# Expert stage of a two-block transformer: weights in whole tiles, four tiles held back in the lead places, and tokens picked by products

## The chip, the cores and the metric

The kernel runs on one core of one Trainium2 chip. The metric is the device time of one execution in microseconds. The core has five engines with instruction streams of their own: TensorE (PE; its weight loads are the rows PEld), VectorE (DVE), ScalarE (ACT), GpSimd (POOL) and SyncE (SP). SyncE and GpSimd issue the transfers here.

## The reference

Two blocks over 256 tokens of width 1024, in float32: HGRN2 and RG-LRU mixing, attention, two feed-forward layers with convolution; then latent attention, a dense SwiGLU, an S5 mixer, and a mixture of experts. Only the last is touched:

```python
def moe_swiglu(h, w_router, w_gate, w_up, w_down):
    t = h.reshape(B * S, D)                        # 256 x 1024
    logits = (t @ w_router).astype(jnp.float32)    # 8 experts
    top_vals, top_idx = lax.top_k(logits, TOP_K)   # TOP_K = 2
    gates = jax.nn.softmax(top_vals, axis=-1)
    combine = jnp.sum(jax.nn.one_hot(top_idx, N_EXPERTS, dtype=jnp.float32) * gates[..., None], axis=1)
    out = jnp.zeros_like(t)
    for e in range(N_EXPERTS):                     # D_FF_EXPERT = 3584
        he = swiglu(t, w_gate[e], w_up[e], w_down[e])
        out = out + combine[:, e:e + 1].astype(t.dtype) * he
    return out.reshape(B, S, D)
```

The input of this step is the RMS norm of the residual with a gain; the residual is added to it, and a last RMS norm with `final_norm` follows.

## The kernel before

Ahead of the experts all weights stream through four slots of 24 KB per partition (`SLOTS`), each unit loaded by SyncE as `slot_free` tells that its slot is empty. The experts follow: each of the 8 has 28 tiles (`FE_TILES`) of 128 hidden channels. A tile has a gate-and-up part of 8 KB per partition (`UP`) and a down part of 4 KB (`DOWN`), 1.5 MB in all, 224 tiles together.

Each token goes to 2 of 8 experts, and an expert computes only the tokens sent to it, at most `CAP` = 88 (if one gets more, a flag `crowded` sends all engines into a dense path, `experts_dense`, that these inputs don't take). TensorE counts each token's place in its expert by products (`router`); VectorE turns this to `posm`, and `picks` makes from it, for one expert, a matrix of 256 x 88 that has the token's inverse norm where token and place agree. `gather` multiplies the tokens `vtok` by it: 32 products of 64 output rows by 88 columns (each appears twice in the trace, so 64 records) leave the chosen tokens in PSUM, transposed as the tiles want them. VectorE's `take_input` scales them to `xg`.

Before the change only experts 0 and 1 get their tokens so, both ahead of the first tile (L1813). For experts 2 to 7, GpSimd scatters all normalized rows (`hrow`, from VectorE, L2743) into a table in HBM, `rows_in`, by four indirect transfers (L573), then loads 88 rows of one expert at a time to `xl` (L567), and TensorE turns them by `turn_rows` (L1826), 32 records, behind the last tile of an expert. `rows_in` is filled with zeros at the program's start (L550, eight stores of 352 KB).

For one tile, `up` (L1866) makes gate and up by 64 records, ScalarE takes Silu of the gate, VectorE multiplies (L2698, `hid_ready`), and `down` (L1882), 32 records, adds into the expert's sums in PSUM, then raises `moe_free`. The order is up of tile f + 1, down of tile f. `four` is four tiles; the first four are written out, the others run in loops. Behind an expert, VectorE copies the sums out (L2705), `open_sums` (L1905) clears them, `turn_sums` (L1835) turns them, and GpSimd stores 88 rows of results to `rows_out` (L583). In the last expert four indirect gathers bring the results back by token (L586, `returned`), and VectorE weighs and adds them.

Where the weights lie: the first four tiles use two of the slots, the lead places. All others go through a ring of four places in the two other slots (`RING`), the up parts and the down parts of a place apart. SyncE refills the up part when `up_ready` tells that its products are done, the down part on `moe_free`:

```python
with sp.Fori(2, last) as i:
    for h in range(RING):
        sp.wait_ge(up_ready, i * (2 * RING) + (2 * (FT0["moe"] + h - RING) + 4))
        load_up((h + 1) % RING, i * RING + (h + 1))
        sp.wait_ge(moe_free, i * RING + h + 1)
        load_down(h, i * RING + h)
```

The lead places hold no further weights afterwards; `hrow`, `xl` and `returned` lie there. Ahead of `gather`, TensorE also spreads the final norm's gains over the partitions by eight products (L1711), and ScalarE copies them out (L1015).

Of the kernel before, what the change touches and what calls it, by code (L numbers as in the profile page):

```python
# [43 lines left out]
RING = 4  # L44
GROUPS = FE_TILES // RING
WEIGHTED_AT = 16
RETURN_AT = 16
ZEROED = 16 * (EXPERTS + 3)
# [120 lines left out]
def build_program(nc, a):  # L169

    ctx = ExitStack()
    with ctx:
# [31 lines left out]
        rows_in = nc.dram_tensor("rows_in", (EXPERTS * T, D), F32, kind="Internal").ap()  # L204
# [59 lines left out]
        def gate_up(f, k):  # L264
# [50 lines left out]
        moe_up_loaded = [sem(f"moe_up_loaded{i}") for i in range(RING)]  # L315
        moe_down_loaded = [sem(f"moe_down_loaded{i}") for i in range(RING)]
# [4 lines left out]
            "scattered", "loaded", "ystored", "returned")}  # L321
# [45 lines left out]
        def mid(k, n):  # L367
# [26 lines left out]
                  for i in (*range(0, 12, 2), *range(20, 34, 2))]  # L394
# [6 lines left out]
        first_picks = [part(i)[:, 0:2 * CAP].rearrange("p (g n) -> p g n", g=2) for i in (22, 23)]  # L401
# [28 lines left out]
        lead_slots, ring_slots = ([(len(LOADED) - SLOTS + k) % SLOTS for k in some]  # L430
                                  for some in ((0, 1), (2, 3)))

        def up_places(two):
            return [slots[two[h // 3]][:, h % 3 * UP:(h % 3 + 1) * UP] for h in range(RING)]

        def down_places(two):
            return [slots[two[1]][:, UP + h * DOWN:UP + (h + 1) * DOWN] for h in range(RING)]

        lead_loaded = [_n[k] + 16 * n for k, n in zip(lead_slots, (3, 1 + RING))]

        lead_ups, lead_downs = up_places(lead_slots), down_places(lead_slots)
        ups, downs = up_places(ring_slots), down_places(ring_slots)

        lead = [slots[k] for k in lead_slots]
        hrow = lead[0][:, 0:2 * D].rearrange("p (g d) -> p g d", g=2)
        xl = lead[0][0:CAP, 2 * D:3 * D]
        returned = lead[1][:, 0:4 * D].rearrange("p (n d) -> p n d", n=4)
        where = part(25)[:, 16:64].rearrange("p (n c) -> p n c", c=8)
        slot_row, back_row = idx[:, 0, 0:4], idx[:, 0, 4:8]
# [6 lines left out]
        def _(sp):  # L456
# [39 lines left out]
            def load_up(h, unit):  # L496
                sp.dma_start(ups[h], a["w_moe"][bass.ds(unit, 1), :, 0:UP].rearrange(
                                 "o p n -> p (o n)")).then_inc(moe_up_loaded[h], 16)
# [17 lines left out]
            for h in range(RING):  # L516
                load_down(h, RING + h)
# [2457 lines left out]
```

## Time and profile before

| | us |
|---|---|
| median of 3 runs | 2178.97 |
| lowest, highest | 2176.01, 2182.1 |
| the profiled execution | 2182.77 |
| its span, first to last instruction | 2180.7 |
| TensorE busy | 2114.9 |
| VectorE busy | 837.9 |
| ScalarE busy | 465.8 |
| GpSimd busy | 24.7 |

The span ends 2.1 us short of the execution's time. The expert stage begins at about 1290 us of the span with the first `gather` and ends near 2168 us, so it is two fifths of the time. Busy times are of the whole span: TensorE is busy 97% of it, which does not tell whether a matmul waited for its weights for a little before each tile. That has to be read from the distance of the starts, and that of the DMA engines from their share in a window.

### The profile page before, as it was taken

What the parts mean: (1) busy time and instruction counts of PE and PEld (TensorE: products, weight loads), DVE (VectorE), ACT (ScalarE), POOL (GpSimd) and SP (SyncE); (2) the same over time, 40 slices, a digit from 0 to 9 for tenths busy, and PEclk for the clock granted to TensorE, in tenths of its full rate; (3) what the DMA queues carried; (4) which work ended last, traced back from release to release, by engine and by line L of the source; (5) the groups of instructions that cost most, each with busy time, mean ns of one, the idle gap of its engine ahead of it and who ended that gap; (6) DMA issues with size and microseconds to landing.
All of it is one profiled execution on the core that took longest, in us unless ns stands there. A gap on an engine that the chain in (4) does not pass through costs nothing.

```text
span 2180.7 us, 67375 instructions
## 1 busy us (share of the span) xinstructions
PE 2114.9 (97%) x30418; PEld 1945.7 (89%) x30418; DVE 837.9 (38%) x2085; ACT 465.8 (21%) x1074; POOL 24.7 (1%) x43
## 2 busy tenths in 40 slices
PE   9999999999999999999997899999999999999998
PEld 8889999856999986899986789999999999999997
DVE  4357676314766655467759520101010101010102
ACT  3432112113311134211023221111111111111112
POOL 1000000000000000000000000000000000000000
PEclk9999999999999999999998999999999999999999
DMA  9241444240334423324431338999999999999997
GB/s 394 93 173 72 162 174 175 81 169 8 139 150 169 160 97 136 155 117 174 168 142 40 116 117 327 413 416 410 418 410 418 409 418 409 418 417 416 418 417 287
DMA packets 78407, 534.35 MB, mean 245 GB/s; under 512 B 9106, under 2 KB 9235, under 8 KB 41939
## 3 DMA queue, kind: packets, MB, share of 16 engines
q1 hardware_dynamic: 74450, 519.82, 59.3%
q0 software_dynamic: 3840, 12.85, 1.6%
q8 instruction: 89, 1.46, 0.3%
q14 instruction: 28, 0.22, 0.0%
HBM read 523.00 MB, written 9.63 MB: 244 GB/s over the span
## 4 chain that ended last, share of the span: by engine, by line
PE 65%; DMA 4%; DVE 2%; ACT 1%; issue 1%; DVEq 0%; SPq 0%; ACTq 0%
PE ps L1866 24%; PE ps L1224 12%; PE ps L1882 11%; PE ps L1266 7%; DMA slot<-in_w_moe 4%; PE ps L1141 4%; PE ps L1633 2%; PE ps L1616 1%; DVE scr L2549 0%; PE ps L1813 0%; PE ps L1157 0%; PE ps L1503 0%; PE ps L1489 0%; PE ps L1096 0%; PE ps L1570 0%
## 5 line engine op out<-in xcount | busy, mean ns | idle before, releaser
L1866 PE MATMUL ps<-scr,slot 128*64 128x88 f32 x14336 | 595.4, 241 | 11.1 <-issue 5.4
L1866 PEld LDWEIGHTS ps<-scr,slot 128*64 128x64 f32 x14336 | 562.8, 137 | 22.1 <-issue 12.4
L2698 DVE TENSOR_TENSOR scr<-scr,ps 128x88 f32<-128x88 f32 x224 | 55.1, 246 | 727.1 <-ACT scr L982 727.1
L1882 PE MATMUL ps<-scr,slot 128*64 128x88 f32 x7168 | 315.5, 239 | 1.9 <-issue 1.9
L1882 PEld LDWEIGHTS ps<-scr,slot 128*64 128x64 f32 x7168 | 292.0, 137 | 5.1 <-issue 5.1
L1266 PE MATMUL ps<-scr,slot 128*128 128x256 f32 x1056 | 237.6, 380 | 1.6 <-DVE scr L2369 1.6
L1266 PEld LDWEIGHTS ps<-scr,slot 128*128 128x128 f32 x1056 | 196.6, 191 | 26.0 <-DVE scr L2369 2.0
L982 ACT ACTIVATE scr<-ps 128x88 f32<-128x88 f32 x224 | 54.5, 243 | 743.8 <-PE ps L1866 743.8
L1224 PE MATMUL ps<-vtok,slot 128*128 128x128 f32 x1056 | 139.6, 275 | 0.0
L1224 PEld LDWEIGHTS ps<-vtok,slot 128*128 128x128 f32 x1056 | 128.8, 192 | 0.2
L1224 PE MATMUL ps<-vtok,proj 128*128 128x128 f32 x1056 | 128.7, 275 | 0.0
L1224 PEld LDWEIGHTS ps<-vtok,proj 128*128 128x128 f32 x1056 | 123.2, 192 | 0.0
L1224 PEld LDWEIGHTS ps<-hT,slot 128*128 128x128 f32 x960 | 116.2, 192 | 2.8
L1224 PE MATMUL ps<-hT,slot 128*128 128x128 f32 x960 | 116.9, 275 | 0.0
L1141 PE MATMUL ps<-hT,slot 128*128 128x256 f32 x416 | 95.7, 389 | 0.6 <-PE ps L1141 0.6
L2295 DVE TENSOR_TENSOR proj<-slot 128x512 f32<-128x512 f32 x132 | 91.1, 690 | 6.2 <-ACT mixT L746 2.9
L839 ACT ACTIVATE sq<-ps 128x128 f32<-128x128 f32 x66 | 18.3, 277 | 351.3 <-PE ps L1224 351.3
L1141 PEld LDWEIGHTS ps<-hT,slot 128*128 128x128 f32 x416 | 80.4, 196 | 13.9 <-issue 3.1
L1320 PE MATMUL ps<-hT,slot 128*128 128x256 f32 x384 | 86.5, 384 | 2.0 <-DMA slot<-in_w_even_in 1.7
L1141 PE MATMUL ps<-mixT,slot 128*128 128x256 f32 x384 | 84.6, 381 | 1.3 <-PE ps L1141 0.9
L1320 PEld LDWEIGHTS ps<-hT,slot 128*128 128x128 f32 x384 | 73.5, 193 | 13.2 <-DMA slot<-in_w_even_in 2.0
L1141 PEld LDWEIGHTS ps<-mixT,slot 128*128 128x128 f32 x384 | 72.5, 190 | 12.9 <-issue 3.0
(412 smaller groups left out, 2058.4 us busy)
## 6 DMA issues: line engine op xcount, KB each, us to landing
slot<-in_w_moe SPq DMA_DIRECT2D x224, 1024.0 KB, 12.2
slot<-in_w_moe SPq DMA_DIRECT2D x224, 512.0 KB, 12.2
slot<-in_w_ffn SPq DMA_DIRECT2D x33, 3072.0 KB, 10.8
slot<-in_w_even_in SPq DMA_DIRECT2D x3, 3072.0 KB, 27.2
slot<-in_w_odd_qk SPq DMA_DIRECT2D x2, 3072.0 KB, 10.6
slot<-in_w_s_glu SPq DMA_DIRECT2D x2, 3072.0 KB, 11.9
slot<-in_w_odd_v SPq DMA_DIRECT2D x2, 2048.0 KB, 8.4
slot<-in_w_even_in SPq DMA_DIRECT2D x2, 1536.0 KB, 10.6
```

Source lines behind the costliest of these rows:

```text
L839: act.activation(mid(k, 0), product(k, P1), ACT.Copy).then_inc(first_copied, 1)
L982: act.activation(gbuf[j][:, 0:CAP], gate_up(j, 0), ACT.Silu).then_inc(gate_act, 1)
L1141: m = pe.matmul(ps[:, bank0 + n % ring, 0:T], w[:, o:o + P], src[:, c], start=c == 0, stop=c == k - 1, skip_group_check=True)
L1224: m = pe.matmul(product(k, n), weights[:, c * P:(c + 1) * P], x[:, c], start=first and c == 0, stop=c == 3, skip_group_check=True)
L1266: m = pe.matmul(acc(d), w[:, o:o + P], hid2[u % 2][:, half], start=u == half == 0 and d % 2 == 0, stop=last, skip_group_check=True)
L1320: m = pe.matmul(even_tile(i), project.w[:, o:o + P], hT[:, c], start=c == 0, stop=c == KD - 1, skip_group_check=True)
L1616: m = pe.matmul(ps[k:k + 32, q % 2, a:b], w[:, r, q, k:k + 32], x[:, j, 0:n], start=False, stop=i == 3, skip_group_check=True)
L1633: m = pe.matmul(glu_tile(i), w[:, o:o + P], hT[:, c], start=c == 0, stop=c == KD - 1, skip_group_check=True)
L1866: m = pe.matmul(gate_up(j, k)[s:s + STRIP], w[:, o:o + STRIP], xg[:, c], start=c == 0, stop=c == KD - 1, skip_group_check=True)
L1882: m = pe.matmul(y_sum(d)[s:s + STRIP], w[:, o:o + STRIP], hid[j][:, 0:CAP], start=False, stop=False, skip_group_check=True)
L2295: dve.tensor_tensor(dst, a, b, ALU.subtract).then_inc(combined, 1)
L2698: dve.tensor_tensor(hid[f % 4][:, 0:CAP], gbuf[f % 4][:, 0:CAP], gate_up(f, 1), ALU.mult).then_inc(hid_ready, 1)
```

## The change

- Both parts of a tile are one transfer of 12 KB per partition (`load_tile`), with one semaphore per place. There are eight places, two in each slot. A place is free when its down products are done (`moe_free`).
- The four lead places (0 to 3) take tiles 0 to 3, and once used, the last four tiles, 220 to 223. The ring (4 to 7) takes all others.
- `gather` serves every expert. VectorE makes the picks for expert e + 2 at the ninth tile of expert e (`PICKS_AT` = 8) in one buffer. `gather` for expert 1 stands behind the first four tiles, the others where `turn_rows` stood.
- `rows_in`, its zeros, the scatter, the loads, `hrow`, `xl` and the row numbers for it are gone. `returned` is spread over four free buffers.
- In the router, four filler products (`busy(4, 5)`) take the place of the eight for the final norm's gains, which stand behind the counting of places; ScalarE copies them after its Exp, and TensorE waits for these copies later.
- The dense path is rewritten for the same places.

```diff
-            for h in range(RING):
-                for s in lead_slots[0:1 if h < 3 else 2]:
-                    sp.wait_ge(slot_free, left(s))
-                sp.dma_start(lead_ups[h], a["w_moe"][h, :, 0:UP]
-                             ).then_inc(slot_loaded[lead_slots[h // 3]], 16)
...
+            def load_tile(h, unit):
+                sp.dma_start(places[h], a["w_moe"][bass.ds(unit, 1), :, :].rearrange(
+                                 "o p n -> p (o n)")).then_inc(moe_loaded[h], 16)
+
+            for h in range(PLACES):
+                sp.wait_ge(slot_free, left(tile_slots[h]))
+                load_tile(h, h)
             for h in range(RING):
...
+                sp.wait_ge(moe_free, RING + h + 1)
+                load_tile(h, TILES - RING + h)
+            with sp.Fori(2, TILES // RING - 1) as i:
                 for h in range(RING):
...
                     sp.wait_ge(moe_free, i * RING + h + 1)
-                    load_down(h, i * RING + h)
+                    load_tile(RING + h, i * RING + h)
...
-            for e in range(EXPERTS):
-                pool.dma_start(rows_in[e * T:e * T + CAP, :], no_rows).then_inc(mo["scattered"], 16)
...
-            for n in range(4):
-                pool.indirect_dma_start(
-                    out=rows_in, out_offset=bass.IndirectOffsetOnAxis(ap=slot_row[:, n:n + 1], axis=0),
-                    in_=hrow[:, n // 2], in_offset=None).then_inc(mo["scattered"], 16)
-            pool.wait_ge(mo["scattered"], ZEROED + 16 * 4)
-            load(2)
...
-                def turn_rows(loads):
-
-                    pe.wait_ge(mo["loaded"], loads)
...
-                gather(0)
-                gather(1)
-                up(0, None, 1)
+                gather(2, picks_of[0], 0)
+                up(0, 0, 16, 1)
                 open_sums(None)
                 four(0, 0, first=True)
+                gather(4, picks_of[1])
                 with pe.Fori(1, GROUPS) as i:
                     four(0, i)
-                turn_rows(16)
+                gather(6, picks_of[1])
                 open_sums(2)
+                pe.wait_ge(fin["rowtaken"], 2)
                 turn_sums(2)
...
-                with pe.Fori(0, GROUPS - 1) as i:
+                with pe.Fori(0, GROUPS - 2) as i:
                     four(EXPERTS - 1, i)
-                four(EXPERTS - 1, GROUPS - 1, True)
+                four(EXPERTS - 1, GROUPS - 2, before_last=True)
+                four(EXPERTS - 1, GROUPS - 1, last=True)
...
+                        if e < EXPERTS - 2 and f == PICKS_AT:
+                            dve.wait_ge(mo["gathered"], 2 * (e + 1) + 2)
+                            picks(e + 2, picks_of[1])
```

How this moves instructions, at three places. On TensorE at the stage's start, before: L1711 are the gains' products, L1718 to L1723 count places, L1946 is the branch on `crowded`, L1813 is `gather`, L1866 the first tile.

```order
L1711 MATMUL ps<-cst,vec 128x128 x8
L1718 MATMUL ps<-scr,cst 128x16
L1721 MATMUL ps<-scr,ones 128x8 x2
L1723 MATMUL ps<-scr,ones 128x8
L1946 TENSOR_LOAD crowded
L1946 ISA x2
L1946 COMPARE_AND_BRANCH
L1813 MATMUL ps<-scr,vtok 64x88 x64
L1866 MATMUL ps<-scr,slot 64x88 x32
```

The same place in the changed kernel, where L1074 are the filler products, L1671 the gains' and L1761 is `gather`.

```order
L1074 MATMUL ps<-cst,ones 128x256 x4
L1663 MATMUL ps<-scr,cst 128x16
L1666 MATMUL ps<-scr,ones 128x8 x2
L1668 MATMUL ps<-scr,ones 128x8
L1671 MATMUL ps<-cst,vec 128x128 x8
L1877 TENSOR_LOAD crowded
L1877 ISA x2
L1877 COMPARE_AND_BRANCH
L1761 MATMUL ps<-scr,vtok 64x88 x32
L1798 MATMUL ps<-scr,slot 64x88 x32
```

The gains' products moved between the counting and the branch, and 32 products of `gather` stand ahead of the first tile in place of 64. On TensorE between the last tile of an expert and the next expert's loop, before: L1826 is `turn_rows`, L1905 `open_sums`, L1835 `turn_sums`.

```order
L1913 COMPARE_AND_BRANCH
L1826 MATMUL ps<-cst,slot 64x88 x16
L1905 MATMUL ps<-cst 128x1 x2
L1835 MATMUL ps<-cst,scr 88x128 x8
L1918 UNCONDITIONAL_BRANCH
```

The same in the changed kernel.

```order
L1843 COMPARE_AND_BRANCH
L1761 MATMUL ps<-scr,vtok 64x88 x32
L1835 MATMUL ps<-cst 128x1 x2
L1771 MATMUL ps<-cst,scr 88x128 x8
L1849 UNCONDITIONAL_BRANCH
```

16 products that read the loaded rows became 32 that read the tokens and the picks. On SyncE's queue, the expert weights up to the ring's loop and its first turn, before (ring slots 3 and 0).

```order
L507 DMA slot1<-in_w_moe 128x2048 [waits slot_free] x3
L507 DMA slot2<-in_w_moe 128x2048 [waits slot_free]
L510 DMA slot2<-in_w_moe 128x1024 x4
L497 DMA slot3<-in_w_moe 128x2048 [waits slot_free] x3
L497 DMA slot0<-in_w_moe 128x2048 [waits slot_free]
L501 DMA slot0<-in_w_moe 128x1024 x4
L497 DMA slot3<-in_w_moe 128x2048 [waits up_ready]
L521 UNCONDITIONAL_BRANCH
L521 ISA
L497 ISA [waits up_ready]
L497 DMA slot3<-in_w_moe 128x2048
L501 ISA [waits moe_free]
```

And in the changed kernel.

```order
L488 DMA slot1<-in_w_moe 128x3072 [waits slot_free] x2
L488 DMA slot2<-in_w_moe 128x3072 [waits slot_free] x2
L488 DMA slot3<-in_w_moe 128x3072 [waits slot_free] x2
L488 DMA slot0<-in_w_moe 128x3072 [waits slot_free] x2
L488 DMA slot1<-in_w_moe 128x3072 [waits moe_free] x2
L488 DMA slot2<-in_w_moe 128x3072 [waits moe_free] x2
L497 UNCONDITIONAL_BRANCH
L497 ISA
L488 ISA [waits moe_free]
L488 DMA slot3<-in_w_moe 128x3072
```

Every load after the first eight now waits for `moe_free` alone, and the four for the lead places (slots 1 and 2) stand ahead of the ring's.

## Rows read from the trace of the kernel before

**Rows 1.** The page: span, and the expert weights among the DMA issues (KB, us to landing).

```profile
span 2180.7 us, 67375 instructions
...
slot<-in_w_moe SPq DMA_DIRECT2D x224, 1024.0 KB, 12.2
slot<-in_w_moe SPq DMA_DIRECT2D x224, 512.0 KB, 12.2
```

**Rows 2.** Windows: stretch, length, busy PE PEld DVE ACT POOL, clock, DMA share, GB/s.

```profile
1300.00:1304.00 4.00, 4.00 (x98) 3.88 (x96) 0.25 (x1) 0.49 (x2) 0.00 (x0) 1.00 0.01 4
1400.00:1500.00 100.00, 98.31 (x2546) 97.44 (x2544) 9.41 (x32) 15.32 (x33) 1.05 (x2) 1.00 1.02 414
```

**Rows 3.** Timeline of TensorE in expert 1: start, us, then line and operation.

```profile
1428.75 2.66 PE L1866 MATMUL ps<-scr,slot 128*64 128x88 f32 x64
...
1494.27 2.66 PE L1866 MATMUL ps<-scr,slot 128*64 128x88 f32 x64
```

**Rows 4.** The chain that ended last, in order of time, in expert 5: start, us.

```profile
1917.10 2.65 PE ps L1866 x64
...
1947.23 2.65 PE ps L1866 x64
```

**Rows 5.** Timeline of VectorE: the copies of an expert's sums, five of eight ends.

```profile
1409.46 0.96 DVE L2705 COPY scr<-ps 128x440 f32<-128x440 f32 x2 [3.95 <-PE ps L1882]
...
1842.77 0.95 DVE L2705 COPY scr<-ps 128x440 f32<-128x440 f32 x2 [4.02 <-PE ps L1882]
...
1951.14 0.96 DVE L2705 COPY scr<-ps 128x440 f32<-128x440 f32 x2 [4.01 <-PE ps L1882]
...
2058.25 0.95 DVE L2705 COPY scr<-ps 128x440 f32<-128x440 f32 x2 [3.95 <-PE ps L1882]
...
2167.58 0.62 DVE L2705 COPY scr<-ps 128x440 f32<-128x440 f32 x1 [1.91 <-PE ps L1882]
```

**Rows 6.** Timeline of TensorE around the end of expert 0.

```profile
1401.71 2.65 PE L1866 MATMUL ps<-scr,slot 128*64 128x88 f32 x64
...
1409.24 1.39 PE L1826 MATMUL ps<-cst,slot 88*64 88x88 f32 x32
1410.56 0.61 PE L1905 MATMUL ps<-cst 128*128 128x1 f32 x4
...
1415.70 2.60 PE L1866 MATMUL ps<-scr,slot 128*64 128x88 f32 x64
```

**Rows 7.** Timeline of TensorE: stalls; in brackets the idle time and its end.

```profile
1329.09 0.24 PE L1866 MATMUL ps<-scr,slot 128*64 128x88 f32 x1 [2.48 <-issue]
...
1426.72 1.05 PE L1866 MATMUL ps<-scr,slot 128*64 128x88 f32 x21 [1.02 <-issue]
...
2086.41 2.65 PE L1866 MATMUL ps<-scr,slot 128*64 128x88 f32 x64 [2.25 <-DMA slot<-in_w_moe]
```

**Rows 8.** Transfers: SyncE's first weights; their landings; window 8:14; 1500:1510; a lone load.

```profile
2.67 0.56 SPq L463 DMA_DIRECT2D slot<-in_w_even_in  x1
3.28 0.47 SPq L464 DMA_DIRECT2D slot<-in_w_even_in  x1
...
DMA to landing us min/median/max: 9.0/9.0/9.0
...
DMA to landing us min/median/max: 12.1/12.1/12.1
...
DMA packets 226, 2.58 MB, mean 430 GB/s; under 512 B 16, under 2 KB 16, under 8 KB 16
...
DMA to landing us min/median/max: 12.1/12.2/12.2
...
slot<-in_w_mla_uk SPq DMA_DIRECT2D x1, 1024.0 KB, 4.8
```

**Rows 9.** The two picks ahead of the first tile, and a window in them.

```profile
1290.21 7.96 PE L1813 MATMUL ps<-scr,vtok 128*64 128x88 f32 x128 [1.76 <-DVE scr L2663]
...
1290.00:1292.00 2.00, 1.79 (x24) 1.80 (x26) 1.50 (x8) 1.77 (x3) 0.00 (x0) 0.50 1.03 422
```

More of the change, by code:

```diff
@@ L320, in build_program @@
             "yetaken", "yturned", "yeready", "spread", "weighted", "pturned", "rows",
-            "scattered", "loaded", "ystored", "returned")}
+            "scattered", "ystored", "returned")}
         out_turned, out_stored = sem("out_turned"), sem("out_stored")
@@ L428, in build_program @@
         mix0 = {"even_out": 0, "odd_out": KD, "mla_o": 2 * KD}
[L430 to L447, printed above, removed]
+        tile_slots = [(len(LOADED) - SLOTS + h // 2) % SLOTS for h in range(PLACES)]
+        places = [slots[s][:, h % 2 * (UP + DOWN):(h % 2 + 1) * (UP + DOWN)]
+                  for h, s in enumerate(tile_slots)]
+        ups, downs = [x[:, 0:UP] for x in places], [x[:, UP:UP + DOWN] for x in places]
+        returned = [yT[:, 4:8].rearrange("p a n -> p (a n)"),
+                    xbp[:].rearrange("p a n -> p (a n)")[:, 0:D],
+                    rgw[:].rearrange("p k j n -> p (k j n)"), part(34, 4)]
         where = part(25)[:, 16:64].rearrange("p (n c) -> p n c", c=8)
-        slot_row, back_row = idx[:, 0, 0:4], idx[:, 0, 4:8]
+        back_row = idx[:, 0, 4:8]
         no_rows = mixT[0:CAP, 0:4].rearrange("p a n -> p (a n)")
@@ L516, in _ @@
-            for h in range(RING):
-                load_down(h, RING + h)
-            last = EXPERTS * FE_TILES // RING - 1
-            sp.wait_ge(up_ready, 2 * (FT0["moe"] + RING) + 2)
-            load_up(0, 2 * RING)
-            with sp.Fori(2, last) as i:
+            def load_tile(h, unit):
[4 more added lines that the diff above has]
+                load_tile(h, h)
@@ L1709, in router @@
                 pe.wait_ge(tile_taken, TILE0["s5_glu"] + 2 * KD)
-                for c in range(KD):
-                    m = pe.matmul(ps[:, 6 + c // 4, c % 4 * P:c % 4 * P + P],
-                                  v("final_norm", c).to_broadcast([P, P]), ident, start=True, stop=True,
-                                  skip_group_check=True)
-                    if c % 4 == 3:
-                        m.then_inc(fin["row"], 1)
+                busy(4, 5)
                 pe.wait_ge(mo["sel"], 2)
@@ L1789, in expert @@
                         down(f)
-                expert(0, True)
-                with pe.Fori(1, EXPERTS) as e:
-                    expert(e, False)
+                expert(0, first=True)
+                with pe.Fori(1, EXPERTS - 1) as e:
+                    expert(e)
+                expert(EXPERTS - 1, last=True)
                 pe.wait_ge(moe_free, RING + EXPERTS * FE_TILES)
@@ L1803, in experts_gathered, with gather @@
             def experts_gathered():
-                def gather(e):
-                    pe.wait_ge(mo["pick"], 2 * e + 2)
+                def gather(picks, picked, bank0=2):
+                    pe.wait_ge(mo["pick"], picks)
                     for b in range(2):
```

169 lines of the change are left out of this document (62 added, 107 removed).

## The prediction

> **What bounds the kernel now.** I read the page first: a span of 2180.7 us, and 224 tiles of expert weights, each in two transfers of 1024 and 512 KB that take 12.2 us to land [rows 1]. The table of windows then shows the expert stage: TensorE busy 98.3 of 100 us and the DMA engines at share 1.02 with 414 GB/s in the same stretch, while from 1300 to 1304 us, when the stage has begun, they move nothing (share 0.01) [rows 2]. So two limits lie on top of each other, and the question is which one is late where. The timeline of TensorE answers it. Where the weights are there, a tile (16 column blocks of gate and up, 8 of down) starts every (1494.27 - 1428.75) / 18 = 3.64 us [rows 3]. Later, in the chain that ended last, eight tiles take 1947.23 - 1917.10 = 30.13 us, 3.77 us each [rows 4]. 1.573 MB in 3.766 us is 417.6 GB/s: there the weight stream sets the pace, 0.126 us a tile above TensorE's own. The copies of an expert's sums, one at each expert's end, give the periods: (2058.25 - 1409.46) / 6 = 108.13 us in the mean for experts 1 to 6, 107.11 for expert 6 alone, 108.37 for expert 5, and 109.33 for the last [rows 5]. The 3.64 us pace alone would be 28 x 3.64 = 101.9.
>
> The rest of a period is the pause between experts and stalls. The pause: three tiles around it take 1415.70 - 1401.71 = 13.99 us, 3.07 more than 3 x 3.64 [rows 6]; of that the turning of the loaded rows (L1826, 32 records) takes 1.32, from 1409.24 to 1410.56 with the next line's start. The stalls: TensorE sits with nothing awaited (the page's "issue") for 1.02 us at 1426.7 and 2.48 us at 1329.1, both in the first tiles after the code leaves one piece and enters another, and 2.25 us for a weight tile at 2086.4, just after the four gathers of returned rows were issued [rows 7].
>
> **The weight stream, part by part.** Before, a period moves 28 tiles, one load and one store of 88 rows. Expert 6's period (107.11) has no load, expert 5's (108.37) has: 352 KB on the GpSimd queue cost 1.26 us of stream [rows 5]. 28 x 3.766 + 2 x 1.26 = 108.0 against the mean of 108.13: these periods are the stream's. 
>
> After: no loads of rows. And a tile is one transfer with 12 KB for each partition in place of 8 + 4. What that does to the rate, the trace shows only nearby: the two first loads, 1536 KB each with 12 KB per partition, were issued at 2.67 and 3.28 us and landed 9.0 and 12.1 us later [rows 8], so at 11.67 and 15.38, 3.71 us apart. That bounds it from above at 3.71; the window from 8 to 14 us, with big packets only, has 430 GB/s [rows 8], 3.66 us a tile. If nothing changes, it stays 3.77; as the lowest I allow 3.62, an estimate 1% under the window. I take 3.67, next to the window, since its packets are the big ones and nothing else is in it.
>
> **The ring.** Before, the gate-up part of a place was refilled as soon as its products were done. From there to its next use lie 4 x 3.64 - 2.43 = 12.1 us, and in the paced stretch a load takes 12.1 to 12.2 us to land [rows 8]: the window is used up exactly. After, the whole place waits for the down products, and its next use comes two tiles later, 7.28 us. A lone 1024 KB load lands in 4.8 us [rows 8]; 512 KB more at 418 GB/s make 6.1, with 0.2 to issue 6.3. The slack is 1.0 us. Hence the stream can't be more than 1 us ahead after an expert's pause, and whatever it falls behind by more, TensorE waits for. The Trainium skill's same page ("Anatomy of one DMA") has a fixed 2.0 us plus bytes / 436e3, an estimate of 5.6 us and 0.5 us more slack; the landings speak for 6.1.
>
> **TensorE, part by part.** The products that pick tokens (L1813) replace the turning of rows: 64 records against 32. At the start 128 of them took 7.96 us [rows 9], but at a granted clock of 0.50, that is 1.2 GHz, after an idle of 1.76 us. Records of the same shape (64 columns by 88) in a tile take 2.43 / 64 = 0.038 us each at full clock, so a pick is 2.43, and the pause grows by 2.43 - 1.2 = 1.2 us, to 4.3. I take that, with 3.98 as the other end (a pick at half clock). It happens behind experts 0 to 5; VectorE writes the picks at the ninth tile, two small operations for each, and is busy only 9.4 of 100 us in the stage [rows 2], so they are there long before. The pick for expert 1 also moves, from ahead of the first tile to behind the fourth: 2.43 there.
>
> Now by stretch:
> - *Stage start to the end of expert 0*, 1290.21 to 1409.46, 119.25 us: 7.8 of picks, 101.9 of tiles, 0.6 of opening, 8.9 of stalls, among them the 2.48. After: one pick at the start instead of two (-3.98), but the eight products of the final norm's gains now stand ahead of the register load and the branch, which used to run within the 1.76 us that TensorE idled for the picks (between 0 and +1.76, taken as +1.2); half clock reaches into the first tile (+1.0); the pick for expert 1 (+2.43). The scatter and its 2 MB fall away, yet the stream, which moved nothing from 1300 to 1304 us [rows 2], is full from the first freed place on, and instructions are fetched beside it; I give 2.4 of the 8.9 back, between 0 and 6. Sum -1.8 (from -5.4 with full clock and few stalls to +1.6).
> - *Six periods to the end of expert 6*: TensorE 101.9 + 4.3 + stalls of about 1.0 (one like that of 1.02 us in expert 1 for each, between 0 and 2 of them) = 107.2. Stream: 28 x 3.67 + 4.3 - 1.0 of slack = 106.1, plus 1.26 for the store, of which a part falls into the stall, 106.7. They lie close and do not overlap fully: 107.4. Six make 644.4 against 648.79: -4.4 (from -8 at 3.62 to +1 at 3.72).
> - *The last expert*: the picks' growth doesn't apply, the turning of the placement stays. 109.33 is 101.9 + 3.1 + 2.25 for the wait on the returned rows and 2.1 of pace. After: the wait stays, the pace goes but for 0.03 x 20 = 0.6 over the tiles ahead of the last four, which lie in place already, and the stall of 1.0 that the old pace hid may show in part or not. Between -2.8 and 0, I take -2.1.
> - *Elsewhere*: the eight stores of zero rows at 26 us at the program's start go; the weights needed then were ahead of them on the rings, so nothing. The gain rows' copy on ScalarE moves behind Exp, and ScalarE has nothing to do until the first tile's gate. The four returned buffers lie elsewhere in SBUF, no cost. The stage's end, 2167.6 to 2180.7, stays.
>
> Sum -1.8 - 4.4 - 2.1 = -8.3 us. The execution profiled took 2182.77, 3.8 above the median of 2178.97 and 2.1 above its span; I put the difference on the median: 2170.7, **2171 us** (a span near 2172.4). What is odd here: an earlier stream in bigger packets and no row loads is worth little, since TensorE's own work is only 1 to 2 us a period shorter than the stream's before, and the picks take most of that back.
>
> **The rivals.**
> *Shallow ring, no faster packets (slower).* If a tile still takes 3.77, then the period is 28 x 3.766 + 4.3 - 1.0 = 108.7, and some of the store on top, 109.0: +0.9 in six, +5.4; the first stretch +1.5, the last expert 0 to +0.5. In all +7, 2186. It decides from 3.72 us a tile on, where 28 x 3.72 + 3.3 + 0.7 gives the present 108.1. For it: 12 KB packets beside a full TensorE appear nowhere. Against: 3.71 and 430 GB/s. Chance 0.13.
> *Everything cancels.* Stalls for code grow, since the loops are entered over more straight code, and each late tile costs in full at 1 us of slack: +1.2 a period instead of a gain of 0.7, first stretch +1: near 2179. Chance 0.20.
> *Stalls mostly vanish.* They came while the stream was full; after the change it often rests, above all in the pauses. Then 106.3 a period (-11), first stretch -4, last -3: 2161. Chance 0.17.
> *The ring isn't rearranged as said* (a tile waits for lead places): the order rows show the lead places refilled ahead of the ring's first, which delays tile 8 only if four loads take longer than four tiles, 14.7 against 14.6 + 2.4. No case of its own.
>
> **How the numbers follow.** Forecast 0.50, around 2171 (its own range 2164 to 2178). 0.3% is 6.5 us, about what a measurement of this kernel can tell from no change: faster is below 2172.4, slower above 2185.5. Of the forecast's half, 0.31 lies below and 0.19 within; with 0.17 of the vanishing stalls faster is 0.48; within 0.19 + 0.18 + 0.03 = 0.40; slower 0.10 + 0.02 = 0.12. The range takes the forecast and both near rivals and reaches to the slow one: 2160 to 2186.
>
> **What would show it.** Right: landings of 1536 KB at 6 to 7 us, DMA share in the stage near 0.97 to 1.0, tiles 3.64 us apart in every expert, periods of 107 to 108 us with a pause of 4.3, first tile near 1296. Wrong: tiles 3.75 apart and waits on the weights after each pause (the slower rival), picks at 0.062 us a record (half clock in the pauses), or many idles without a releaser.

## The result, and the profile after

The changed kernel takes 2263.05 us (median of 4, 2259.01 to 2267.0) where the kernel before, beside it on the chip, takes 2178.21: a ratio of 1.0387, 95% interval 1.0361 to 1.0414. It is slower by 85 us, far outside the range; the slow rival had the right sign with a tenth of the size.

The page of the changed kernel. From section 1's head, section 4, section 5 and section 6, the lines that answer to [rows 1]; the last two columns of section 5's line are the busy time with the mean of one in ns, and the idle time ahead of them with what ended it:

```profile
span 2263.8 us, 67094 instructions
...
L1798 PE MATMUL ps<-scr,slot 128*64 128x88 f32 x14336 | 590.7, 240 | 74.2 <-DMA slot<-in_w_moe 70.3
...
slot<-in_w_moe SPq DMA_DIRECT2D x224, 1536.0 KB, 8.4
```

TensorE sat idle for 70.3 us for expert weights; before it was 4.1. The rest of the 83.1 us of span is mostly in its busy time, which grew by 18.4 us, from 2114.9 to 2133.3: behind a wait the first part of a tile takes 2.65 us in place of 2.43, as the chain below shows. The waits of TensorE in the stage (us in total, times, longest) and the windows that answer to [rows 2]:

```profile
PE ps L1798 <- DMA slot<-in_w_moe: 70.3, 96, 2.0
```

```profile
1400.00:1500.00 100.00, 91.44 (x2288) 88.23 (x2284) 9.14 (x31) 12.03 (x28) 0.52 (x1) 1.00 0.94 364
```

96 small waits, none above 2.0 us, and the stream at 364 GB/s where [rows 2] had 414. The DMA engines' share is 0.94: they are neither full nor resting for long. This points at a ring that is too shallow, not at a stream that is too heavy; the experiments test it. The landings, first of the three loads issued at 1303.6, 1307.2 and 1310.8 us (the first, into an empty queue, took 6.7 us, the next two 8.2 and 9.3), then of the 23 issued from 1400 to 1500 (they answer to [rows 8]):

```profile
DMA to landing us min/median/max: 6.7/8.2/9.3
```

```profile
DMA to landing us min/median/max: 7.7/8.4/10.1
```

The chain of waits in expert 0 (start, us) shows what a refill costs TensorE, from the issue to the first product:

```profile
1323.81 2.43 PE ps L1798 x64
...
1331.26 8.71 DMA slot<-in_w_moe
...
1340.02 2.65 PE ps L1798 x64
...
1344.05 8.29 DMA slot<-in_w_moe
```

Timeline of VectorE, the copies of an expert's sums, as in [rows 5] (experts 0, 6 and 7):

```profile
1420.78 0.95 DVE L2634 COPY scr<-ps 128x440 f32<-128x440 f32 x2 [4.95 <-PE ps L1809]
...
2135.42 0.95 DVE L2634 COPY scr<-ps 128x440 f32<-128x440 f32 x2 [4.03 <-PE ps L1809]
...
2250.69 0.62 DVE L2634 COPY scr<-ps 128x440 f32<-128x440 f32 x1 [1.90 <-PE ps L1809]
```

So the loss by stretch, the third column being an experiment below (gate-up part refilled early):

| stretch, us | before | after | early refill |
|---|---|---|---|
| program's start to the first copy | 1409.46 | 1420.78 | 1408.89 |
| six periods | 648.79 | 714.64 | 638.55 |
| one of them | 108.13 | 119.11 | 106.43 |
| last expert | 109.33 | 115.27 | 107.95 |
| from there to the end | 13.1 | 13.1 | 13.1 |

79% of the loss, 65.85 of 83.1 us, lies in the six periods, 11 us in each. Last, TensorE at the stage's start and around the end of expert 0, as in [rows 9] and [rows 6]:

```profile
1290.11 2.03 PE L1671 MATMUL ps<-cst,vec 128*128 128x128 f32 x16
1292.07 2.65 PE L1761 MATMUL ps<-scr,vtok 128*64 128x88 f32 x64
1296.54 0.68 PE L1798 MATMUL ps<-scr,slot 128*64 128x88 f32 x12 [1.83 <-DVE scr L2611]
...
1420.57 2.60 PE L1761 MATMUL ps<-scr,vtok 128*64 128x88 f32 x64
1423.10 0.60 PE L1835 MATMUL ps<-cst 128*128 128x1 f32 x4
1423.56 1.05 PE L1771 MATMUL ps<-cst,scr 128*88 128x128 f32 x8
1424.55 2.65 PE L1798 MATMUL ps<-scr,slot 128*64 128x88 f32 x64
```

Behind expert 0 the pick runs at full clock and takes 2.53 us to the next line's start, where the turning took 1.32: 1.2 us more, as forecast. From the pick's first product to the next expert's tile are 3.98 us. What failed is the ring.

### The profile page after: what moved, and what is told of

It is laid out like the page before. It is cut to its first block, busy times and chain, and to the rows that moved or that the text cites. A ratio compares the mean times of both kernels' runs of the same rounds, so it can differ in the third digit from the quotient of the medians.

```text
span 2263.8 us, 67094 instructions
## 1 busy us (share of the span) xinstructions
PE 2133.3 (94%) x30618; PEld 1951.5 (86%) x30618; DVE 838.1 (37%) x2094; ACT 466.1 (21%) x1074; POOL 13.4 (1%) x25
## 4 chain that ended last, share of the span: by engine, by line
PE 47%; DMA 22%; DVE 3%; ACT 1%; issue 1%; SPq 0%; DVEq 0%; ACTq 0%
DMA slot<-in_w_moe 22%; PE ps L1798 12%; PE ps L1174 11%; PE ps L1216 7%; PE ps L1809 6%; PE ps L1091 4%; PE ps L1583 2%; PE ps L1761 1%; PE ps L1566 0%; DVE scr L2480 0%; PE ps L1771 0%; PE ps L1107 0%; PE ps L1453 0%; PE ps L1439 0%; PE ps L1520 0%
## 5 line engine op out<-in xcount | busy, mean ns | idle before, releaser
L1798 PE MATMUL ps<-scr,slot 128*64 128x88 f32 x14336 | 590.7, 240 | 74.2 <-DMA slot<-in_w_moe 70.3
L1798 PEld LDWEIGHTS ps<-scr,slot 128*64 128x64 f32 x14336 | 555.2, 137 | 100.0 <-DMA slot<-in_w_moe 66.7
L1809 PE MATMUL ps<-scr,slot 128*64 128x88 f32 x7168 | 310.2, 239 | 0.9 <-issue 0.9
L1809 PEld LDWEIGHTS ps<-scr,slot 128*64 128x64 f32 x7168 | 287.4, 137 | 1.0 <-issue 1.0
L1091 PE MATMUL ps<-hT,slot 128*128 128x256 f32 x416 | 95.4, 388 | 0.7 <-PE ps L1091 0.7
L1270 PE MATMUL ps<-hT,slot 128*128 128x256 f32 x384 | 91.4, 399 | 2.6 <-DMA slot<-in_w_even_in 2.3
L1091 PEld LDWEIGHTS ps<-mixT,slot 128*128 128x128 f32 x384 | 72.4, 190 | 13.1 <-issue 3.0
```

The lines of the kernel that those rows point to most:

```text
L1091: m = pe.matmul(ps[:, bank0 + n % ring, 0:T], w[:, o:o + P], src[:, c], start=c == 0, stop=c == k - 1, skip_group_check=True)
L1270: m = pe.matmul(even_tile(i), project.w[:, o:o + P], hT[:, c], start=c == 0, stop=c == KD - 1, skip_group_check=True)
L1798: m = pe.matmul(gate_up(j, k)[s:s + STRIP], ups[place][:, o:o + STRIP], xg[:, c], start=c == 0, stop=c == KD - 1, skip_group_check=True)
L1809: m = pe.matmul(y_sum(d)[s:s + STRIP], downs[place][:, o:o + STRIP], hid[j][:, 0:CAP], start=False, stop=False, skip_group_check=True)
```

## The experiments

Three theories stood against each other. **A**: the ring is too shallow: too few bytes are in flight, since a place's window, from its refill to its next use, is too short. **B**: transfers of whole tiles in 12 KB rows are slower in themselves. **C**: TensorE's side, picks or code. All times are medians; "ratio" is against the kernel before, run beside it (2176.6 to 2178.4).

### A deeper ring, and the same ring held back

All eight places become one ring; nothing is special about the first or the last four tiles.

```
+            with sp.Fori(1, TILES // PLACES) as i:
+                for h in range(PLACES):
+                    sp.wait_ge(moe_free, i * PLACES + (h - RING + 1))
+                    load_tile(h, i * PLACES + h)
```

TensorE's code has the place of a tile follow from its number modulo eight, so loops of eight tiles are written out in place of four. The two held-back kernels differ from it in one constant, `+ 4` or `+ 5` for `+ 1`.

> The changed kernel with one edit in the order of the weight transfers: the eight places are one ring for all 224 tiles, so a freed place is needed again six tiles later (21.8 us) and not two (7.28 us); transfers stay whole tiles of 12 KB rows, picks stay products. Theory A (too few transfers in flight: a tile's transfer lands 8.2 to 8.4 us after its issue with one other in flight, two tiles per landing make 4.2 us a tile): with six in flight the stream runs at 3.7 to 3.77 us a tile, the periods fall from 119 to 107-109 us and the time to 2150-2180. Theory B (whole-tile transfers with 12 KB rows are slower in themselves): the rate stays at 360 to 390 GB/s, periods stay above 115, time 2230-2265. Theory C (TensorE's side: picks, code): above 2200 with no waits on the weights. My number: 2165.

> The ring of eight places, but each refill waits for four more tiles to be done, so that a place is needed again two tiles after its transfer is issued, as in the changed kernel; nothing else differs from the ring of eight. Theory A: the periods come back to 118-122 us, time 2250-2275 (2263). Theory B: the same as the ring of eight without the wait, whatever that is. Theory C: the same as that too.

> The ring of eight places with refills held back by three tiles: a place is needed again three tiles (10.9 us) after its issue. Theory A: up to three transfers in flight; before, 3.24 tiles in flight made 3.77 us a tile; if landings go as 3 x the tile time, the stream runs at 3.7 to 3.85, periods 108-111, time 2170-2195 (2180). Theory B: the same as the ring of eight. Theory C: the same.

Measured: the ring of eight 2231.92 (ratio 1.0246, 1.0226 to 1.0266), held back by four tiles 2292.63 (1.054, 1.0503 to 1.0577), by three 2226.72 (1.0228, 1.0205 to 1.0251). The first line of TensorE's waits in the stage, of the one held back by four and of the one by three:

```profile
PE ps L1790 <- DMA slot<-in_w_moe: 62.0, 84, 1.9
```

```profile
PE ps L1790 <- issue: 31.3, 25, 5.0
PE ps L1801 <- issue: 18.2, 17, 1.9
```

One tile more of window, 3.64 us, takes 84 waits on weights down to none and 66 us off the time. Code, picks, places and packets are the same in both, so A holds and B falls. With three tiles of window the stream also runs as fast as it can, in the window 1585 to 1625 of the kernel held back by three:

```profile
1585.00:1625.00 40.00, 40.00 (x1062) 40.00 (x1060) 2.71 (x11) 6.54 (x14) 0.00 (x0) 1.00 1.01 426
```

426 GB/s is 3.69 us a tile; the tiles there start 3.64 us apart. But the time I gave, 2165, was missed by 67 us. A new cost had come in with my edit: 31 + 18 us of idle in which TensorE waits for nothing the profile shows. That is taken up below.

### Which part of the ring's change does it

The ring of four was changed in two ways: both parts are refilled at the tile's end, and both are waited for at the tile's start. Four kernels separate the two, with the picks of the changed kernel, and one does the refill alone in the kernel before. First, the changed kernel with two transfers on one semaphore, so that only the packets are those of before:

```
-                sp.dma_start(places[h], a["w_moe"][bass.ds(unit, 1), :, :]...
+                sp.dma_start(ups[h], a["w_moe"][bass.ds(unit, 1), :, 0:UP]...
+                sp.dma_start(downs[h], a["w_moe"][bass.ds(unit, 1), :, UP:UP + DOWN]...
```

> The changed kernel with each tile brought by two transfers (1024 KB in 8 KB rows, 512 KB in 4 KB rows) issued together when its place is free, and waited for together: the changed kernel's window with the packets of before. Theory A (the window alone): time 2250-2270, periods 117-121. Theory B (12 KB rows or whole-tile transfers): back to 2170-2190. Mixed: if the shorter packets spread a tile more evenly over the queue, 2230-2250. My number: 2255.

Measured 2266.01 (ratio 1.0418, 1.0388 to 1.0448), the changed kernel's time. B falls a second time, and from the other side. Next, the same refill with the parts waited for apart:

```
-                def down(j, place, hids):
+                def down(j, place, hids, loads):

+                    if place >= RING:
+                        pe.wait_ge(moe_down_loaded[place], loads)
```

> The changed kernel with the gate-up and the down part of the four ring places brought apart and waited for apart, both refilled together when the place's down products are done. Against the kernel with both parts on one wait (2266 us) only the wait for the down part moves, from ahead of the tile's gate-up products to ahead of its down products, 6.07 us later (two gate-up parts and one down part, 2.43 + 1.21 + 2.43). If the one wait is what costs, the down third of the bytes gains 6.07 us of window (13.35 in place of 7.28) and the time falls to 2172-2190 (2178), as the kernel before with the late refill alone (2187) less the 8.5 us that picks and missing row transfers are worth. If the refill at the tile's end is what costs, 2240-2266.

Measured 2190.62 (1.0052, 1.0034 to 1.0069). Then the early refill, with both waits as before:

```
+                    sp.wait_ge(up_ready, i * (2 * RING) + (2 * (FT0["moe"] + h - RING) + 4))
+                    load_up(RING + (h + 1) % RING, i * RING + (h + 1))
                     sp.wait_ge(moe_free, i * RING + h + 1)
-                    load_tile(RING + h, i * RING + h)
+                    load_down(RING + h, i * RING + h)
```

> The changed kernel with the gate-up part of the four ring places brought apart (8 KB rows) and refilled as soon as its products are done, the down part (4 KB rows) when the down products are done, as the kernel before does; picks as products, no rows loaded or scattered and the lead places used again for the last four tiles stay. Theory A: the stream is back at 418 GB/s, 3.77 us a tile, periods 28 x 3.77 + up to 1.3 for the store = 105.5-107.5, where TensorE's own 101.9 + 4.3 make 106.2: time 2165-2180 (2170), no long waits on the weights. Theory C (picks or code cost it): above 2200.

Measured 2168.18 (0.9956, 0.9942 to 0.997), 0.4% faster than the kernel before. Its gate-up parts land 8.6 us after their issue, in a stream of 418 GB/s from 1500 to 1900 us:

```profile
slot<-in_w_moe SPq DMA_DIRECT2D x106, 1024.0 KB, 8.6
```

And the early refill with one wait for both parts at the tile's start:

> The changed kernel with both parts of the four ring places apart and the gate-up part refilled early (the kernel of 2168 us), but TensorE waits for both parts ahead of the gate-up products. Window of the gate-up part 12.1 us, of the down part 7.28. If what counts is the window weighted by bytes (here 10.5 us; 9.3 held the pace nearly, 7.28 didn't), little is lost: 2168-2185 (2178). If the shortest window of any part counts, with a tile's landing of 8.4 us, 2220-2265.

Measured 2192.14 (1.0064, 1.0042 to 1.0086). TensorE's waits on the weights in these four, in the order told:

```profile
PE ps L1800 <- DMA slot<-in_w_moe: 68.6, 89, 2.5
```

```profile
PE ps L1818 <- DMA slot<-in_w_moe: 10.9, 13, 2.4
```

```profile
PE ps L1829 <- DMA slot<-in_w_moe: 1.2, 1, 1.2
```

```profile
PE ps L1830 <- DMA slot<-in_w_moe: 8.0, 10, 2.6
```

| | two waits | one wait |
|---|---|---|
| gate-up refilled early | 2168.2 | 2192.1 |
| both refilled at the end | 2190.6 | 2266.0 |

Either edit costs 22 to 24 us, both together 98. They don't add. The late refill takes 4.85 us of window from the gate-up part, the early wait takes 6.07 us from the down part, and only when both are gone has every byte of a tile just 7.28 us. The landings fit this: the part that is left with 7.28 us lands 7.2 us after its issue where it is the gate-up part alone, 7.1 where it is the down part alone, and 8.4 where it is the whole tile. So either part alone just about fits the window and the whole tile doesn't. That is read from the landings; no run varies them by themselves.

What the half edits still cost is the pause. In the middle of an expert their stream runs at its full rate, and behind the pause it doesn't, since it had no free place to run ahead into. Early refill with one wait, ten us in the middle of expert 2 and ten just behind the pause after it:

```profile
1590.00:1600.00 10.00, 9.93 (x262) 9.76 (x259) 0.74 (x3) 2.01 (x4) 0.00 (x0) 1.00 1.02 418
1630.00:1640.00 10.00, 10.00 (x250) 9.81 (x250) 1.78 (x4) 0.49 (x2) 0.51 (x1) 1.00 0.94 339
```

Its periods are 109.6 us in the mean, those of the late refill with two waits 110.3: near 28 x 3.766 + 3.98 = 109.4, a stream that sets the pace in the tiles and rests in the pause. My guess that the window weighted by bytes decides is not borne out: 10.5 us of it (early, one wait) is no faster than 9.3 (late, two waits), and they came out 14 and 13 us slower than I had put them.

The late refill alone, in the kernel before:

```
+            with sp.Fori(2, EXPERTS * FE_TILES // RING) as i:
                 for h in range(RING):
-                    sp.wait_ge(up_ready, i * (2 * RING) + (2 * (FT0["moe"] + h - RING) + 4))
-                    load_up((h + 1) % RING, i * RING + (h + 1))
                     sp.wait_ge(moe_free, i * RING + h + 1)
+                    load_up(h, i * RING + h)
                     load_down(h, i * RING + h)
```

> The kernel before with one edit: the gate-up part of a ring place is refilled together with its down part, when the down products are done, as the changed kernel does, and not as soon as the gate-up products are done. Its window shrinks from 12.1 to 7.28 us; row loads, turned rows, 8 + 4 KB rows stay. Theory A (window): the tile time goes to 4.2 us with two tiles in flight, periods 118-123 us, time 2255-2275 (2265), waits on the weights of 60 us and more; this part of the change alone makes the loss. Theory C (the loss is in picks, code or packets of 12 KB): within 10 us of 2178.

Measured 2186.66 (1.0055, 1.0038 to 1.0071), where I expected 2265: a miss, and the most useful one. I had overlooked that the kernel before waits for the down part only ahead of the down products. Its issues from 1400 to 2000 us (KB, median us to landing) show why it nearly suffices; they stand against a window of 7.28 us for the first part and 13.35 for the second:

```profile
slot<-in_w_moe SPq DMA_DIRECT2D x154, 1024.0 KB, 7.2
slot<-in_w_moe SPq DMA_DIRECT2D x154, 512.0 KB, 7.9
```

The late refill costs 10 us here and 22 where the early-refill kernel is the base. That fits the pace: the kernel before already pays the stream's 3.77 us a tile (its periods for experts 2 to 5 are 108.3 to 109.0 us, with the late refill 107.8 to 108.4), while in the early-refill kernel TensorE's 3.64 decides. So the gains of the two can't be added, as I had done for the 2178 above.

### Where the rings of eight lose their gain

The same ring with less code: one loop of eight tiles, run seven times for two experts, with the work between experts inside it behind a condition.

```
+                with pe.Fori(0, EXPERTS // 2) as q:
+                    with pe.Fori(0, FE_TILES // RING) as m:
+                        four(q, m, 0)
+                        with pe.If(m == 3):
...
+                        four(q, m, 1)
```

> The ring of eight places with less code: one loop body of eight tiles is run 7 times for two experts, the work between the experts stands in it behind a condition on the loop's register, and the pick for expert 1 stands ahead of the first tile. The ring of eight (2232) had no waits on the weights but 55 us of idle with nothing awaited, and 59 to 63 instruction packets in 700 us of its stage against 7 of the changed kernel. If that idle is code being loaded (its body of two experts has 24 tiles written out, the changed kernel's 4), it goes with the smaller body: periods 106-108, time 2150-2170 (2158), instruction packets under 15 in the same stretch. If it isn't the size of the code but the entering of loops: the same 2225-2235. If conditions on TensorE are dear, 1 to 2 us each of 28: 2190-2215.

Measured 2201.76 (1.0121, 1.0104 to 1.0138): 30 us less than the ring of eight, neither of the times expected in full. The idle has shrunk to 30.1 us in nine pieces. Six of them, of 3.8 to 4.9 us, come in pairs each time the outer loop turns back to its start, as here in the chain of waits, with the window behind the first; none stands at the condition.

```profile
1509.83 0.92 PE ps L1763 x8
1510.74 4.89 issue
1515.63 4.96 PE ps L1790 x64
...
1535.94 3.75 issue
```

```profile
1515.00:1521.00 6.00, 5.37 (x74) 5.38 (x76) 0.09 (x1) 0.24 (x1) 0.00 (x0) 0.50 0.21 83
```

The clock granted there is 0.50, and 64 records take 4.96 us in place of 2.65. So a turn costs more than its idle: the periods with a turn are 121.49, 119.76 and 119.29 us, those without 105.96 each. Without the 42.7 us of the three turns this kernel would take an estimated 2159 us, which is what was expected of it.

The instruction queue on the page, for the changed kernel, the ring of eight and this one:

```profile
q8 instruction: 93, 1.52, 0.3%
```

```profile
q8 instruction: 160, 2.62, 0.4%
```

```profile
q8 instruction: 105, 1.72, 0.3%
```

To see whether code alone does this, the inner loop of the 2168 us kernel was written out; TensorE's products, the waits and the transfers stay the same:

```
                 with pe.Fori(1, EXPERTS - 2) as e:
-                    with pe.Fori(0, GROUPS) as i:
+                    for i in range(GROUPS):
                         four(e, i)
```

> The kernel of 2168 us (gate-up part refilled early) with one edit on TensorE alone: for experts 1 to 5 the inner loop of seven rounds of four tiles is written out, 28 tiles of code one behind the other, and run once for each expert. Transfers, waits and products are the same. If TensorE's idle in the rings of eight was the loading of code, its idle grows here too: with every tile's code run once for each expert, either 2 to 4 us at each expert's start only, since straight code is fetched ahead (time 2178-2195), or all along, 1 us and more for each four tiles (2200-2240); instruction packets in 600 us of the stage 100 or more against 7. If that idle had to do with the ring of eight and not with code, the time stays 2165-2171. My number: 2200.

Measured 2287.46 (1.0511, 1.0488 to 1.0534), 119 us slower. TensorE's waits in the stage, the instruction queue in the 400 us from 1500 on (1 packet there in the early-refill kernel), the chain at the end of an expert, and the window behind it:

```profile
PE ps L1829 <- issue: 82.1, 61, 4.8
```

```profile
q8 instruction: 73, 1.20, 1.2%
```

```profile
1531.21 1.47 issue
1532.69 2.04 PE ps L1789 x48
1534.73 0.54 PE ps L1868 x4
1535.26 0.91 PE ps L1799 x8
1536.18 4.49 issue
1540.67 4.64 PE ps L1829 x64
```

```profile
1541.00:1545.00 4.00, 4.00 (x62) 4.00 (x60) 0.00 (x0) 0.00 (x0) 0.00 (x0) 0.52 0.01 4
```

The periods of experts 1 to 5, whose loop was written out, are 124.7 to 135.4 us; those of experts 6 and 7, whose loops stayed, are 107.8 and 107.2. So the idle without a releaser is TensorE waiting for its code: mostly 1 to 1.5 us every few tiles where each tile's code is new, 4 to 5 where the loop turns back. After the long ones the clock has fallen too, to 0.52 in the window from 1541 to 1545 us, and 64 records take 4.64 us in place of 2.65. I had expected a quarter of it. The Trainium skill's page "Runtime: NRT & Kernel Launch", section "Instruction fetch mechanics", has room for 2048 of TensorE's instructions, refilled in blocks of 16 KiB, and a stall where a branch leaves what is loaded. The trace agrees: 1.20 MB in 73 packets are 16.4 KB each, and with a weight load and a product for each record a loop of four tiles has 768 instructions and runs free of idle once it is entered, 28 tiles have 5376 and don't. The section calls the streaming of long straight code mostly hidden; here it cost the 97 us of idle, and the measurement decides. This explains why no ring of eight reached 2165, and it isn't a part of the changed kernel's loss, whose stage has one such wait above 1 us.

Last, the rows alone, with a deep ring: the compact ring of eight with 8 + 4 KB rows.

> The ring of eight places with one loop body (2202 us), each tile brought by two transfers (8 + 4 KB rows) on one semaphore in place of one with 12 KB rows; window six tiles in both. Only the rows differ. If 12 KB rows give the stream its 427 GB/s (3.68 us a tile) against 418 (3.77), windows in the middle of a pair of experts show 418 and tiles 3.64 apart only while the stream is ahead: time 2202-2212 (2206), since the idle between experts lets the stream run ahead by six tiles. If the rows make no difference, 427 GB/s and 2202.

Measured 2199.78 (1.0099, 1.0079 to 1.0119), as with 12 KB rows (2201.76). Windows from 1585 to 1625 with 12 KB rows, and with 8 + 4 KB:

```profile
1585.00:1625.00 40.00, 40.00 (x1061) 40.00 (x1058) 3.57 (x13) 6.37 (x14) 0.00 (x0) 1.00 1.01 427
```

```profile
1585.00:1625.00 40.00, 40.00 (x1060) 40.00 (x1058) 2.71 (x11) 5.97 (x14) 0.00 (x0) 1.00 1.02 418
```

The longer rows do give the stream 2%, 3.68 us a tile against 3.76. It is worth nothing to the time here: neither kernel waits for weights, and their periods without a turn are the same 105.96 us, TensorE's own.

## Why the prediction was wrong, step by step

**The ring: the step that failed.** The window of 7.28 us was right; the landing put against it, 6.1 us and 0.2 to issue, wasn't. It was a lone transfer's, scaled up from [rows 8], and in this ring a transfer is never alone: while one is under way, the next is issued 4 us later. Measured are 8.4 us in the stage, and even the one issued into an empty queue took 6.7. The Trainium skill's page "DMA: Bandwidth & Descriptors", section "Anatomy of one DMA", has a formula, fitted on transfers that GpSimd issues, that would have made it an estimated 5.6 us; the landings of SyncE's transfers here are 1.1 us above that into an empty queue and 2.8 us with a neighbour.

How that becomes 11 us a period can be worked out. From the end of a place's down products to its next use there are four tile times t, less the tile itself from its first product to its last, 7.28 us, stretched by one wait of t - 3.64: 4t - 7.28 - (t - 3.64) = 3t - 3.64. With 6.3 us from issue to use t could be 3.31, so TensorE's 3.64 decides; that is the slack of 1.0 us in the prediction. With 8.4 + 0.2 it is t = 12.24 / 3 = 4.08 us. 28 x 4.08 and a pause of 3.98 make 118.2, against the measured 119.11. A landing 2.3 us later than forecast, 0.98 of it slack, so costs (2.3 - 0.98) / 3 = 0.44 us in each of 28 tiles. The prediction treated the slack as something the stream lives on after a pause; it is a condition on every tile.

**What was said and not used.** [Rows 8] have 12.1 to 12.2 us for a landing in the kernel before, and I read it as the window used up. It says as well that 12.2 / 3.77 = 3.2 tiles were in flight when the stream ran at 418 GB/s, and the change allowed two. That was a warning, though it overstates the need: there the stream set the pace and its queue filled the window. The early-refill kernel has the same windows and runs at the same 418 GB/s, but TensorE sets its pace, and its landings are 8.6 us, 2.3 tiles in flight. The window's doses bear the warning out: two tiles of it give 358 to 376 GB/s, three 426.

**The forgotten wait.** The prediction counted the early refill's loss for the gate-up part. The second half of the change, that the whole tile must be there before the first gate-up product, took 6.07 us from the down part's window, and no term of the sum has it. By the table above it costs as much as the other, 24 us alone and 75 on top of the late refill.

**The rate of 12 KB rows.** Taken at 3.67 us a tile, between 3.62 and 3.77: measured 3.68 and 3.69 where the ring is deep. Right, and of no use, since the changed kernel never gets there.

**The price of a row transfer.** The prediction read 1.26 us for 352 KB from one period with a load against one without, and that it tells 11 engines from 16 (0.86 us). It can't: the five periods before that have both a load and a store lie between 107.48 and 108.99 us. And the early-refill kernel moves 28 tiles and a store in 105.95 us; 28 x 3.766 leave 0.5 us for the store. So no run shows the 1.26.

**TensorE's part.** The kernel with the early refill shows it undisturbed. The copies of its sums, for experts 0, 6 and 7:

```profile
1408.89 0.96 DVE L2667 COPY scr<-ps 128x440 f32<-128x440 f32 x2 [3.75 <-PE ps L1842]
...
2047.44 0.95 DVE L2667 COPY scr<-ps 128x440 f32<-128x440 f32 x2 [3.75 <-PE ps L1842]
...
2155.39 0.62 DVE L2667 COPY scr<-ps 128x440 f32<-128x440 f32 x1 [1.91 <-PE ps L1842]
```

The pause is 3.98 us for pick, opening and turning, where 4.3 was forecast: the pick's 1.2 us more were right, but the 3.07 us they were added to held 0.3 us of the stream's pace (turning, opening and turning of sums alone were 2.77 us, from 1409.24 to 1412.01). Periods of 106.43 stand against the 107.4 forecast. Of TensorE's 107.2 in that sum, 1.0 was a stall for code in each period: this kernel's periods 2 to 5 are 105.95 us, 28 x 3.64 and the pause, with no stall at all. The last expert took 107.95, 1.4 less than before; the forecast had 2.1 less, but its own terms, 2.1 of pace less 0.6 that stays, give 1.5 at most.

The first tile of the changed kernel came at 1296.54 (forecast near 1296), and that was luck. The clock was full at the pick, not half, so the pick took 1.3 us less than the 3.98 put for it. It began 1.9 us later than before, behind 2.03 us of gains' products (0.8 later in the early-refill kernel, where the same code stands; the forecast had 1.2). And behind it TensorE waited 1.83 us for the picked tokens, which VectorE scales (L2611); no term had this wait. Before, the second pick ran in that time. The pick for expert 1 cost 2.6 us plus an idle that was not in the sum, in the changed kernel's chain from 1314.95 on:

```profile
1314.95 2.27 PE ps L1761 x60
1317.22 2.51 issue
1319.73 0.37 PE ps L1761 x4
```

**The total.** Picks, no row transfers and the reused lead places are worth 8.5 us with the ring as it was (2168.18 against 2176.67), which is the size the prediction gave to the whole change; the ring's new order takes 95. That the 8.3 us are met so is luck: this kernel has the old rows and none of the faster stream, and by stretch its profile shows -0.6, -10.2 and -1.4 us where -1.8, -4.4 and -2.1 stood. Its periods are those of the rival in which the stalls mostly vanish (106.3), not the forecast's.

**The rivals.** The slow one named the ring, but as a matter of the rate: "it decides from 3.72 us a tile on". The rate that 12 KB rows can reach was on the good side of that, and the kernel was slower all the same. What this rival describes, a tile of 3.77 us and a stream that can't use the pause, is what the two half edits show: periods of 109.6 and 110.3 us and times of 2192 and 2191, against its 109.0 and 2186. Of the signs given, landings of 6 to 7 us and a share near 1.0 were to show it right; 8.4 and 0.94 show it wrong, at the first two places to look.

**Left open.** Why a transfer lands 8.4 us after its issue with one neighbour, when 6.7 into an empty queue and 3.7 for the neighbour's share would leave it at about 6.7 at a distance of 4.1 us. The windows hint at dearer bytes in a queue that runs dry (share 0.94 at 364 GB/s, 1.01 at 427: 9% more engine time for a byte), but no run tested it.

## What to carry to other kernels

Before a buffer is given fewer or later refills, write down each part's window, from where it may be refilled to where it is first waited for, and set it against a landing seen under load, not a lone transfer's. Merging two transfers into one moves both ends of the window, and the whole lands later than either part. Where the landing is longer, the ring sets the pace on every tile; where it just fits, the stream still can't run ahead, and every pause is lost to it. A landing read where the stream sets the pace (12.2 us here) holds its queue as well and overstates the need: with the same windows and the same rate it was 8.6 us once TensorE set the pace. A deeper ring that needs more written-out code can pay it all back in code loading: keep the inner loop's body small, and look at the instruction queue's packets.

## What the runs showed of the hardware

- Longer rows: 12 KB rows gave 426 to 427 GB/s, 8 + 4 KB rows 418, with six tiles of window in both compact rings of eight and the DMA share at 1.01 and 1.02.
- Depth: 1.5 MB transfers with two tiles of window ran at 358 to 376 GB/s with landings of 8.4 us, with three tiles at 426. With 8 + 4 KB rows 418 GB/s were held with landings of 12.2 us (before) and of 8.6 (early refill).
- Code: TensorE fetching 28 tiles' code once for each expert lost 97 us to idle in the stage, with 73 instruction packets in 400 us against 1. A loop body of four tiles ran free of it once entered (periods of 105.95 us); the compact body of eight lost mostly where its outer loop turned back, 13 to 16 us a turn, with the clock at 0.50 behind the idle. Straight code wasn't fetched far enough ahead to hide it.
